# Mix of the heads in a two-layer trunk kernel: reciprocals by TensorE, one transfer per tile, cast on ScalarE, first output tiles ordered by column third

## What is computed

```python
mla_out = block_attention(q_full, k_mla, v_mla, MLA_QK_DIM ** -0.5).reshape(b, s, MLA_WIDTH)
fnet_out = jnp.fft.fft2(uf, axes=(1, 3), norm='ortho').real.reshape(b, s, FNET_WIDTH)
gqa_out = block_attention(gq5, gk_all, gv_all, GQA_HEAD_DIM ** -0.5).reshape(b, s, GQA_WIDTH)
out = jnp.concatenate([mla_out, fnet_out, gqa_out], axis=-1) @ w_out
...
x = x + gate1 * mix
h = rms_norm(x, g2) * (1 + scale2) + shift2
x = x + gate2 * ((jax.nn.silu(h @ w_gate) * (h @ w_up)) @ w_down)
```

## Time and profile before

| what | value |
|---|---|
| three runs | median 3910.36 us (3908.92 to 3916.11) |
| the profiled execution, its own time | 3910.42 us |
| its span | 3908.5 us |
| mean granted TensorE clock | 0.937 |
| PE busy | 88% of the span |
| DVE busy | 45% |
| POOL busy | 23% |
| ACT busy | 18% |

### The profile page before, as it was taken

One profiled execution on the slowest core, in us unless ns is written; L12 is line 12 of the kernel. 1 busy time (PEld: TensorE's weight loads), 2 busy tenths in 40 slices (PEclk: granted clock), 3 DMA queues, 4 the chain that ended last, 5 costly groups with the idle time before them and its releaser, 6 DMA issues.

```text
span 3908.5 us, 48884 instructions
## 1 busy us (share of the span) xinstructions
PE 3444.0 (88%) x17432; PEld 2965.7 (76%) x17432; DVE 1765.8 (45%) x2750; ACT 719.8 (18%) x1286; POOL 882.3 (23%) x526
## 2 busy tenths in 40 slices
PE   6697489996869999999959884999958799999998
PEld 3696445553869999999949862555548799999998
DVE  1404766665253433433360176666642633433343
ACT  2212333332030000000031131333311200000001
POOL 1421011111342222222142101111121422222220
PEclk9897789998989999999979896999979899999999
DMA  5113833432301111111002257333241111111111
GB/s 176 56 59 106 268 102 116 117 99 76 88 28 38 38 43 43 43 43 42 23 26 86 76 185 199 94 105 116 71 118 41 33 43 43 43 43 43 43 32 48
DMA packets 315300, 301.94 MB, mean 77 GB/s; under 512 B 67402, under 2 KB 262004, under 8 KB 315172
## 3 DMA queue, kind: packets, MB, share of 16 engines
q1 hardware_dynamic: 285220, 263.21, 23.3%
q10 hardware_dynamic: 29952, 37.17, 2.6%
HBM read 250.55 MB, written 49.90 MB: 77 GB/s over the span
## 4 chain that ended last, share of the span: by engine, by line
PE 78%; DVE 9%; issue 7%; SPq 3%; DMA 2%; ACT 1%; DVEq 0%; ACTq 0%
PE ps L1500 20%; PE ps L1502 20%; PE ps L1501 20%; PE ps L1732 8%; PE ps L1752 4%; DVE neg_max L1352 3%; PE ps L1541 2%; SPq L501 1%; DVE h_hi L1163 1%; PE ps L1772 1%; PE ps L1717 1%; PE ps L1716 1%; SPq L663 1%; PE ps L1526 1%; SPq L664 1%
## 5 line engine op out<-in xcount | busy, mean ns | idle before, releaser
L1500 PE MATMUL ps<-h_hi,w_hi 128*128 128x384 f32 (+1 forms) x3072 | 1064.6, 347 | 224.5 <-DVE h_lo L1165 134.4
L1501 PE MATMUL ps<-h_lo,w_hi 128*128 128x384 f32 (+1 forms) x3072 | 1050.2, 342 | 0.0
L1502 PE MATMUL ps<-h_hi,w_lo 128*128 128x384 f32 (+1 forms) x3072 | 1049.2, 342 | 0.0
L1500 PEld LDWEIGHTS ps<-h_hi,w_hi 128*128 128x128 f32 (+1 forms) x3072 | 585.5, 191 | 238.7 <-issue 107.8
L1501 PEld LDWEIGHTS ps<-h_lo,w_hi 128*128 128x128 f32 (+1 forms) x3072 | 585.1, 190 | 8.0
L1502 PEld LDWEIGHTS ps<-h_hi,w_lo 128*128 128x128 f32 (+1 forms) x3072 | 584.3, 190 | 3.2
L1440 DVE SCALAR_TENSOR_TENSOR x<-ps,lmod,x 128x384 f32<-128x384 f32 (+2 forms) x768 | 366.3, 511 | 332.6 <-PE ps L1502 332.6
L1464 DVE TENSOR_TENSOR wk<-ps,wk 128x384 f32<-128x384 f32 x132 | 73.6, 558 | 850.0 <-PE ps L1502 845.6
L829 POOL CAST w_hi<-w_stage 128x1024 fp32r<-128x1024 f32 x120 | 124.7, 1039 | 1070.0 <-PE ps L1502 707.2
L1025 ACT ACTIVATE p_t<-ps 128x512 f32<-128x512 f32 (+1 forms) x456 | 264.5, 580 | 505.3 <-PE ps L1502 265.9
L1500 PE MATMUL ps<-act_hi,w_hi 128*128 128x384 f32 x1056 | 356.9, 338 | 0.0
(11 more groups left out here) (244 smaller groups left out, 4184.7 us busy)
## 6 DMA issues: line engine op xcount, KB each, us to landing
ada_buf<-in_w_ada SPq DMA_DIRECT2D x96, 512.0 KB, 7.2
w_stage<-in_w_ffn_gate SPq DMA_DIRECT2D x44, 512.0 KB, 3.9
w_stage<-in_w_ffn_up SPq DMA_DIRECT2D x44, 512.0 KB, 3.8
w_stage<-in_w_ffn_down SPq DMA_DIRECT2D x44, 512.0 KB, 3.6
s_in<-ev_p ACTq DMA_DIRECT2D x66, 192.0 KB, 1.9
w_stage<-in_w_in SPq DMA_DIRECT2D x24, 512.0 KB, 4.0
ada_w<-in_w_ada SPq DMA_DIRECT2D x4, 2048.0 KB, 17.0
w_stage<-in_w_out SPq DMA_DIRECT2D x16, 512.0 KB, 5.1
```

The source lines that it names most:

```text
L1500: nc.tensor.matmul(out, wh, xh, start=first, stop=False)
L1501: nc.tensor.matmul(out, wh, xl, start=False, stop=False)
L1502: return nc.tensor.matmul(out, wl, xh, start=False, stop=last)
```

## The change

`s_o` becomes a tensor of 12 x 64 rows, and the sums get a tensor of their own, `s_sum`. Two transfers store what one stored, and one transfer of 128 rows fetches an attention tile. The first four tiles are fetched before the last two stores of attention are made.

The reciprocals no longer go to DRAM. PE spreads them: `rc_rows(q)` multiplies, for attention tile `q`, six times a column of the identity matrix, repeated 64 times, by the 108 x 128 reciprocals (two heads by three blocks of 128 tokens). That gives the 128 x 384 factors in PSUM, in bank 4 or 6 by turns. Seven of the 18 `rc_rows` of a layer stand ahead of the output projection and eleven between its first output tiles. Each attention tile's turn waits until DVE has multiplied the tile two turns earlier (`mix_norm`).

DVE multiplies by PSUM, ACT casts to `h_hi` (a new loop ahead of `norm_x`), and DVE subtracts, one tile behind. DVE's modulation vectors move behind the mix loop.

The first twelve output tiles are ordered third by third: four channel tiles of the first third, then four of the second, four of the third. From the thirteenth on the order is as before. Three of the five weight units of `w_out` that were loaded behind the mix tiles are now loaded among them. The context transposes move from tile 6 to tile 9.

```diff
+OUT_FIRST = 4
+RC_BANK = (4, 6)
+N_RC = G * (DK - 2)
+def out_tile(n):
+    return (n % OUT_FIRST, n // OUT_FIRST) if n < OUT_FIRST * G else divmod(n, G)
+def rc_after(n):
+    return range(DK - 1 + 3 * n, min(DK + 2 + 3 * n, N_RC)) if n < OUT_FIRST else range(0)
...
@@ SP, store_o
-                    sp.dma_start(s_o[row, :, c0:c0 + w], o_n[0:VD + 1, n % 2, 0:w]).then_inc(o_stored[n % 2], 16)
+                    sp.dma_start(s_o[row * VD:(row + 1) * VD, c0:c0 + w], o_n[0:VD, n % 2, 0:w])\
+                        .then_inc(o_stored[n % 2], 16)
+                    sp.dma_start(s_sum[row:row + 1, c0:c0 + w], o_n[VD:VD + 1, n % 2, 0:w])\
+                        .then_inc(o_stored[n % 2], 16)
...
@@ SP, load_mix and behind it
-                    for half, h in enumerate(head_rows(k)):
-                        r0 = 64 * half
-                        sp.dma_start(wk[r0:r0 + 64, i % 4, :], s_o[h, 0:VD, cols(g)]).then_inc(mix_loaded[i % 4], 16)
-                        sp.dma_start(rc[r0:r0 + 64, i % 4, :], s_rec[h:h + 1, cols(g)].to_broadcast([64, GW]))\
-                            .then_inc(mix_loaded[i % 4], 16)
+                    src = s_fnet[(k - 3) * P:(k - 2) * P] if is_fnet(k) else \
+                        s_o[head_rows(k)[0] * VD:(head_rows(k)[0] + 2) * VD]
+                    sp.dma_start(wk[:, i % 4, :], src[:, cols(g)]).then_inc(mix_loaded[i % 4], 16)
...
+                for i in range(4):
+                    load_mix(i)
+                store_o(2 * HEADS - 1, 1)
+                store_o(2 * HEADS - 1, 2)
...
+                sp.dma_start(sums[0:108, 0, :], s_sum.rearrange("h (a b) -> (h a) b", b=P)).then_inc(sums_loaded, 16)
+                for i in range(4, G * DK):
                     load_mix(i)
-                sp.wait_ge(rec_done, l + 1)
-                sp.dma_start(s_rec.rearrange("h (a b) -> (h a) b", b=P), sums[0:108, 1, :]).then_inc(rec_stored, 16)
-                sp.wait_ge(rec_stored, (l + 1) * 16)
...
+                    if i in (7, 11, 15):
+                        m = STAGES + (i - 7) // 4
+                        load_unit(U_OUT + m, w_out_v[l, :, :, m * P:(m + 1) * P], P)
...
@@ ACT, ahead of norm_x
+                for i in range(G * DK):
+                    g, k = i // DK, K_ORDER[i % DK]
+                    if is_fnet(k):
+                        act.wait_ge(mix_loaded[i % 4], l * MIX_LOADS[i % 4] + MIX_AFTER[i])
+                    else:
+                        act.wait_ge(mix_norm, l * G * DK + normed(i))
+                    nc.scalar.activation(h_hi[:, k, cols(g)], wk[:, i % 4, :], ACT.Copy).then_inc(mix_hi, 1)
@@ DVE, behind the reciprocal
+                def mix_low(i):
+                    g, k = i // DK, K_ORDER[i % DK]
+                    dve.wait_ge(mix_hi, l * G * DK + i + 1)
+                    nc.vector.tensor_tensor(h_lo[:, k, cols(g)], wk[:, i % 4, :], h_hi[:, k, cols(g)].bitcast(F32),
+                                            ALU.subtract).then_inc(mix_split, 1)
+
+                for i in range(G * DK):
+                    g, k = i // DK, K_ORDER[i % DK]
+                    dve.wait_ge(mix_loaded[i % 4], l * MIX_LOADS[i % 4] + MIX_AFTER[i])
+                    if not is_fnet(k):
+                        q = rc_index(i)
+                        dve.wait_ge(rc_mm, l * N_RC + q + 1)
+                        nc.vector.tensor_tensor(wk[:, i % 4, :], wk[:, i % 4, :], ps[:, RC_BANK[q % 2], 0:GW], ALU.mult)\
+                            .then_inc(mix_norm, 3 if i % DK == DK - 1 else 1)
+                    if i:
+                        mix_low(i - 1)
+                mix_low(G * DK - 1)
                 dve.wait_ge(late_ev, (l + 1) * NHEADS)
...
@@ PE
+                def rc_rows(q):
+                    g, k = q // (DK - 2), K_ORDER[q % (DK - 2) + 2]
+                    if q >= 2:
+                        pe.wait_ge(mix_norm, l * G * DK + normed(rc_tile(q - 2)))
+                    for j in range(3):
+                        row = head_rows(k)[0] * 9 + 3 * g + j
+                        for h in range(2):
+                            sel = ident[0:108, row + 9 * h:row + 9 * h + 1].to_broadcast([108, VD])
+                            ins = nc.tensor.matmul(ps[VD * h:VD * (h + 1), RC_BANK[q % 2], j * P:(j + 1) * P], sel,
+                                                   sums[0:108, 1, :], start=True, stop=True)
+                    ins.then_inc(rc_mm, 1)
+
+                pe.wait_ge(rec_done, l + 1)
+                settle(pe)
+                for q in range(DK - 1):
+                    rc_rows(q)
...
-                        m, g = divmod(n, G)
+                        m, g = out_tile(n)
...
+                    for q in rc_after(n):
+                        rc_rows(q)
```

More of the change, by code:

```diff
@@ L157, in head_rows, with rc_index, rc_tile, normed @@
     return (2 * k, 2 * k + 1) if k < 3 else (2 * k - 4, 2 * k - 3)
+OUT_FIRST = 4
[3 more added lines that the diff above has]
+    return (n % OUT_FIRST, n // OUT_FIRST) if n < OUT_FIRST * G else divmod(n, G)
+def rc_index(i):
+    return i // DK * (DK - 2) + i % DK - 2
+def rc_tile(q):
+    return q // (DK - 2) * DK + q % (DK - 2) + 2
+def normed(i):
+    return i + 1 if i % DK == DK - 1 else i - 1
+def rc_after(n):
+    return range(DK - 1 + 3 * n, min(DK + 2 + 3 * n, N_RC)) if n < OUT_FIRST else range(0)
 MIX_LOADS, MIX_AFTER = [0] * 4, []
 for _i in range(G * DK):
-    MIX_LOADS[_i % 4] += 16 * (1 if is_fnet(K_ORDER[_i % DK]) else 4)
+    MIX_LOADS[_i % 4] += 16
     MIX_AFTER.append(MIX_LOADS[_i % 4])
@@ L667, in _ @@
+                    sp.dma_start(wk[:, i % 4, :], src[:, cols(g)]).then_inc(mix_loaded[i % 4], 16)
+                sp.wait_ge(k_low, l * NHEADS + NHEADS - 1)
+                settle(sp)
                 for i in range(2):
-                    sp.wait_ge(o_stored[i], (l + 1) * (NHEADS * GROUPS // 2 * 16))
+                    sp.wait_ge(o_stored[i], l * (NHEADS * GROUPS // 2 * 32) + 4 * GROUPS // 2 * 32)
                 settle(sp)
-                sp.dma_start(sums[0:108, 0, :], s_o[:, VD, :].rearrange("h (a b) -> h a b", b=P))\
-                    .then_inc(sums_loaded, 16)
+                for i in range(4):
+                    load_mix(i)
@@ L676, in _ @@
-                sp.wait_ge(rec_stored, (l + 1) * 16)
-                settle(sp)
-                for i in range(2, G * DK):
-                    load_mix(i)
+                    if i in (7, 11, 15):
+                        m = STAGES + (i - 7) // 4
+                        load_unit(U_OUT + m, w_out_v[l, :, :, m * P:(m + 1) * P], P)
                 sp.dma_start(ctx_in[:, 0:2, :], s_cc.rearrange("(k p) t -> p k t", p=P)).then_inc(ctx_loaded, 16)
@@ L684, in _ @@
                     .then_inc(ctx_loaded, 16)
-                for m in range(STAGES, N_OUT):
+                for m in range(STAGES + 3, N_OUT):
                     load_unit(U_OUT + m, w_out_v[l, :, :, m * P:(m + 1) * P], P)
@@ L1422, in _ @@
                 link(gain_and_scale(1))
-                for i in range(G * DK):
-                    g, k = i // DK, K_ORDER[i % DK]
-                    dve.wait_ge(mix_loaded[i % 4], l * MIX_LOADS[i % 4] + MIX_AFTER[i])
-                    if not is_fnet(k):
-                        n = l * (G * (DK - 2)) + g * (DK - 2) + i % DK - 1
-                        nc.vector.tensor_tensor(wk[:, i % 4, :], wk[:, i % 4, :], rc[:, i % 4, :], ALU.mult)\
-                            .then_inc(mix_norm, 1)
-                        dve.wait_ge(mix_norm, n)
-                    nc.vector.tensor_copy(h_hi[:, k, cols(g)], wk[:, i % 4, :]).then_inc(mix_hi, 1)
-                    dve.wait_ge(mix_hi, l * G * DK + i + 1)
-                    nc.vector.tensor_tensor(h_lo[:, k, cols(g)], wk[:, i % 4, :], h_hi[:, k, cols(g)].bitcast(F32),
-                                            ALU.subtract).then_inc(mix_split, 1)
                 def add_gated(m, g, gate, bank, done):
@@ L1808, in _ @@
                     if n < G * DK:
-                        m, g = divmod(n, G)
-                        if g == 0:
-                            wh, wl = unit(U_OUT + m, P)
+                        m, g = out_tile(n)
+                        wh, wl = unit(U_OUT + m, P) if g == 0 else wtiles(U_OUT + m, P)
                         if m == 0:
```

29 lines of the change are left out of this document (12 added, 17 removed).

## The result

The changed kernel took 3874.57 us (median of five runs, 3868.27 to 3890.44), the kernel before 3908.92 (five runs, 3904.49 to 3916.11). The ratio is 0.9917, 95% interval 0.9889 to 0.9945: 34 us faster by the medians, between 21 and 43 by the interval. The prediction was 3891, with 3872 to 3907. The profiled execution took 3874.57 us, its span 3872.8 (before 3908.5), at a mean granted clock of 0.941 (before 0.937).

What follows compares the result with a forecast made beforehand. PE, busy 88% of the span, bounds the kernel; its waits for mix tiles were 90.1 us. Terms sum to 63.4 us a layer against 73.05, 19.3 saved in all: 3910.4 to 3891 us, range 3872 to 3907.

Steps and rivals of the forecast that it cites:

- turns of 0.7: Spreading of reciprocals on PE: a turn of 0.7 us instead of 1.4 would show the forecast wrong.
- rival 1: Spreading turns: two heads run side by side in the array, 0.7 us a turn, 9.2 a layer less, 3873; chance 0.18.
- start of the first output tile: From attention's end to the projection's first output tile: 20.6 us, 25.5 before; 20 to 21 named as sign of being right.
- four output tiles, one cold: First third's output tiles: 4 x 4.2 = 16.8 us, plus 2.9 for one tile slowed by the clock.
- eleven turns: Later spreading turns between output tiles, hidden by nothing: 11 x 1.4 = 15.4 us a layer.
- new wait ahead of the fifth: Fifth output tile waits for the first gated addition, behind DVE's mix tiles and modulation vectors: 3.5 us.
- fifth tile: The fifth output tile, end point of the compared stretch: 4.2 us at 2.4 GHz.
- if load and stream lie beside each other a turn of 12 records takes 12 x 0.115 = 1.4 us: Price of one spreading turn on PE, weight loads hidden beside streaming: 1.4 us; 2.7 if they follow each other.
- Rival 2: Late subtraction before first output tile meets POOL's split, 2.58 for 0.56; both gaps slow a tile: 3901; chance 0.15.
- rival 4: Start: the seven turns stay at 1.2 GHz, 2.6 each, first tile 5 us later, 3901; chance 0.05.
- I price one layer and double it: Both layers' mix: layer 1 begins like layer 0, so 9.65 us gained a layer makes 19.3.
- At nothing: Second stores, first loads, early weight units, later POOL slots, later context transposes: no cost; uncovered, a few us each.

Runs made afterwards that it cites:

- one_head: The change with each turn spreading only the first head of a pair (part of the result left out): three turns 2.38 us, change 2.40.
- wide_columns: The change with one 128-column matmul per block instead of two of 64: three turns 2.23 us; attention's end to fifth tile's end 57.53 and 57.13.
- low_first: The change with DVE's last subtraction of a third before the wait for the next third's load: attention's end to fifth tile's end 54.96 and 56.55 us.
- change_again: The changed kernel unaltered, executed again: median 3872.18 us, ratio 0.9921 to the kernel before; attention's end to fifth tile's end 59.78 and 58.68.
- adds_between: The change with modulation vectors and three gated additions moved between DVE's mix tiles: attention's end to fifth tile's end 53.82 and 52.68 us.
- both edits: The change with the earlier last subtraction, and vectors and three additions between mix tiles: median 3859.89 us, ratio 0.9888 to the kernel before.
- no_later_turns: The change without the eleven later spreading turns (part of the result left out): attention's end to fifth tile's end 54.05 and 53.70 us.
- order_undone: The change with output tiles in the order of before, later turns behind the first two tiles: attention's end to fifth tile's end 65.70 and 65.19 us.

## Why the prediction was right, and where it was off

The mechanism of the gain stood: it is the idle time of PE at the start and ahead of the second and third thirds, and a new wait came where it was put. The price of a turn did not: turns of 0.7 were named as a sign of being wrong, and they came; the measured time lies where rival 1 (3873) lies and not at 3891. The first tile's start, 19.6, is also just outside the 20 to 21 that were named. Against the sum of 63.4 us a layer, layer 0 measured 58.57:

| term | put | measured, layer 0 |
|---|---|---|
| start of the first output tile | 20.6 | 19.56 |
| four output tiles, one cold | 16.8 + 2.9 | 20.16 |
| eleven turns | 15.4 | 9.85 (0.90 of it waiting) |
| new wait ahead of the fifth | 3.5 | 3.42 |
| fifth tile | 4.2 | 5.58 |

**The mis-sized term is "if load and stream lie beside each other a turn of 12 records takes 12 x 0.115 = 1.4 us".** A turn took 0.80 us (2.40 for three), which is rival 1, given 0.18. Its price of 0.7 fits the records alone (0.65); the rest of the 2.40 is the third turn's wait of 0.23 for DVE and the way in and out of a group. I counted twelve records of 128 columns as one stream; two of each pair run together, and `one_head` shows that the pair costs what one costs. The Trainium skill ("TensorEngine Tiling", Theoretical Speedup) gives up to a factor of two for this, and the runs agree: 4.07 against 2.40, 1.7 with all that does not shrink, and 1.31 against 0.65 by the records of a turn. The drain at a change of mode that this page of the Trainium skill has under Key Properties would lie within the 0.3 us between `wide_columns` and the change (0.17 in the turns, 0.1 in the tile behind them), five groups a layer; it could not have spoken against the change. The page on TensorE's clock ("TensorE: Matmul & The Clock Gate", LDWEIGHTS, in the Trainium skill), read as load and stream in a row, gave 2.0 a turn; `wide_columns`, with 128 weight columns in 2.23 us for three turns, shows that they lie beside each other.

**Luck in the total.** Rival 1 puts the saving in the mix at 37.7 us, 18.85 a layer, and 30.2 were measured. That its 3873 is so near to 3874.57 owes to the 7.2 us by which the part between the two mixes was shorter, whose visible source is the pace of the feed-forward chunks, which the change does not touch. So the forecast's own miss in the mix is 30.2 against 19.3.

**The start.** The load of the sums went out at 938.55 where I had put 937.4: attention ended 0.8 us later here, and each of the four last stores held SP about 0.5. The reciprocals were ready sooner all the same, 4.6 us after attention for 5.0. The seven turns took 10.3 us (941.42 to about 951.7) for 12.2, and 2.9 of that was waiting for DVE, whose subtractions met POOL's in more places than the two that I counted. Tile 8 did land behind the weights as worked out, and DVE was released by it 18.5 us after attention:

```profile
947.12 2.24 DVE L1460 TENSOR_TENSOR h_lo<-wk,h_hi 128x384 fp32r<-128x384 f32 x1
...
955.16 3.65 DVE L1460 TENSOR_TENSOR h_lo<-wk,h_hi 128x384 fp32r<-128x384 f32 x2 [2.17 <-DMA wk<-s_fnet]
```

`low_first` prices that order at 2.7 to 2.9 us. Errors of both signs cancelled within 1 us. Rival 2's late subtraction came in small: the one that the first tile needs took 1.01 us from 955.16, not 0.56 and not 2.58.

The clock did not set the start. Over the seven turns it was 0.83 here; in layer 0 of `change_again` it stayed at 0.50 through all of them, as rival 4 has it, they took 11.3 us for 10.3, and the first tile started at 19.66 for 19.56. Rival 4 priced a turn at 1.2 GHz at 2.6; at half of that the turns stay ahead of the transfers.

**The new wait** of 3.42 for 3.5 holds two errors that cancel: the copy of the vectors took 0.19 us where 0.8 was put, and DVE was still at an earlier subtraction when the last turn ended.

**The clock.** I charged one cold tile, one that runs at 1.2 GHz for most of its length. There was one of 2.7 (the first) and half of one more: the fifth took 1.3 more than in `adds_between` in layer 0 and 1.5 more in layer 1. In `change_again` it was a whole one in layer 0, 2.8, so rival 2's second slow tile is real in some executions. The stretches of the first tile, of three turns and of the fifth tile, with the granted clock as third number from the end:

```profile
956.22:963.15 6.93, 6.93 (x25) 6.68 (x25) 3.53 (x3) 0.52 (x1) 4.09 (x3) 0.59 0.56 161
963.15:965.55 2.40, 2.33 (x37) 1.92 (x36) 1.41 (x4) 0.52 (x1) 1.49 (x1) 1.00 0.04 7
...
989.65:995.23 5.58, 5.58 (x25) 5.58 (x26) 1.80 (x6) 2.10 (x4) 0.00 (x0) 0.74 0.00 0
```

**"I price one layer and double it"** left out 1.2 us: layer 1 took 74.39 before and 58.67 after. That is no more than the stretch varies between executions.

**"Eleven turns, which nothing hides"** is true of the change and not of the next step: taking them away brings the fifth tile's start forward by 5.8 us of their 9.

**"At nothing": the cast.** I let it lie beside DVE's work and gave it no price of its own. It is worth 8.3 and 6.7 us a layer, as much as the order of the tiles. The terms that were put at nothing in so many words (second stores, early loads, later slots) were not tested one by one; the same 14.5 and 15.7 us at the first activation of the feed-forward part leave no cost of them behind the fifth tile.

## What to carry to other kernels

Before a wait is called a wait for data, look at what is written between the two on the releasing engine: of the two waits that were left here, all of the one ahead of the fifth tile (an addition behind the whole loop of mix tiles) and about half of the one ahead of the first (a subtraction behind a load that it did not need) were waits of order, and moving a few instructions brought 7.4 us a layer. Price small matmuls by whether their outputs fill different column halves of the array, and measure one pair before the sum is made. Where DVE and POOL work at the same time, a pass more on DVE can cost several times its own length, while an idle ScalarE did the same pass at its usual pace.

## What the runs showed of the hardware

- Two f32 matmuls with 64 weight columns and 128 moving columns, on different halves of the PSUM partitions and written one after the other, took the time of one: 2.40 against 2.38 us for three turns, and pairs start 0.109 us apart in both. On the same half they took 4.07.
- A short wait costs more than itself. The fifth tile took 4.27 us behind no wait, at a granted clock of 1.00. Behind waits of 3.1 to 3.4 us (six traces, twelve layers) it took 5.58 to 5.85 in ten layers (clock 0.74 in the stretch of 5.58) and 6.99 and 7.08 in two (clock 0.56 in that of 7.08); behind 7.70 and 8.16 it took 6.87 and 6.62. Equal waits do not cost the same.
- Making the wait ahead of the first tile short (0.95 us, both edits, layer 1) did not save that tile: it took 6.69. The clock was down already: 0.65 over the 11 us of turns with waits between them, and 0.50 over the wait itself.
- DVE's cast of 0.35 us took up to 2.04, and its subtraction of 0.55 up to 2.75, while POOL was splitting weights; DVE's product with PSUM as an operand kept 0.54 to 0.56 in the same microseconds, and ACT's cast 0.51 to 0.53.
- The chunk of a layer's feed-forward part takes 75.09 or 76.05 us for all ten full chunks of a layer, at a granted clock of 1.00 in both cases, and which one a layer gets differs between executions of equal code: layer 0 of the profiled execution before, of `no_later_turns` and of `low_first`, and layer 1 of `adds_between` and `order_undone` had 76.05, all others 75.09. That is 9.6 us a layer, more than many an edit, and its cause stays open. Single times of such kernels should be compared by stretches.
